# State-space tables made in the down tiles, chunk inputs two rounds ahead in halves, first steps beside the input product

## The reference, cut to what matters

```python
u = rmsnorm(x) @ odd_w_in                   # the input product ("odin")
lam = min(lam_re, -1e-4) + 1j * lam_im      # 128 groups of 64 states
lam_bar = exp(lam * dt)                     # decay and turn of each state per token
b_bar = (lam_bar - 1) / lam * (b_re + 1j * b_im)
h[t] = lam_bar * h[t-1] + b_bar @ u[t]      # per group, 16 channels in and out
y = real(c @ h) * 2 + d_skip * u
out = gelu(y) * sigmoid(gelu(y) @ w_glu + b_glu)
```

## Time and profile before

| what | value |
|---|---|
| median of 3 runs (range) | 4123.23 us (4119.73 to 4124.74) |
| the profiled execution, device time | 4120.54 us |
| its span, first to last instruction | 4119.2 us, mean granted clock 0.973 |
| busy: PE, DVE, ACT, POOL | 93%, 63%, 43%, 36% |
| chain that ended last: PE, DVE, ACT, DMA | 73%, 16%, 7%, 2% |
| layer 0's net, 2017.9 to 2832.7 us | 814.8 us |
| `odin` and state space, 2832.7 to 3072.3 us | 239.6 us |

### The profile page before, as it was taken

The page is one execution under the profiler, slowest core; times in us unless marked ns, Lnnn a source line. Parts: engine busy times, 40 slices in busy tenths (PEclk is TensorE's granted clock), DMA queues, the critical chain, the costliest instruction groups (busy, mean ns, idle before and its releaser), DMA issues.

```text
span 4119.2 us, 66502 instructions
## 1 busy us (share of the span) xinstructions
PE 3835.4 (93%) x28426; PEld 3256.0 (79%) x28426; DVE 2580.1 (63%) x3607; ACT 1788.5 (43%) x2781; POOL 1472.7 (36%) x701
## 2 busy tenths in 40 slices
PE   6898999999999999989899898999869999999998
PEld 3786888787878887888688786888758878888887
DVE  0435743794378897677777767466555866455457
ACT  1435443654355444545534433344334554333334
POOL 0332443243323440024334343444534434444443
PEclk8999999999999999999999999999889999999999
DMA  9653665345534451034345554547325434454543
GB/s 392 270 213 148 263 232 224 141 166 212 210 143 164 164 199 59 3 144 169 132 162 194 186 202 178 210 184 286 145 104 193 175 143 184 184 186 182 198 178 135
DMA packets 60119, 747.66 MB, mean 182 GB/s; under 512 B 6704, under 2 KB 8880, under 8 KB 16176
## 3 DMA queue, kind: packets, MB, share of 16 engines
q1 hardware_dynamic: 48960, 696.74, 44.4%
q0 software_dynamic: 8800, 44.57, 2.7%
q10 hardware_dynamic: 2064, 2.10, 0.1%
HBM read 726.60 MB, written 16.78 MB: 180 GB/s over the span
## 4 chain that ended last, share of the span: by engine, by line
PE 73%; DVE 16%; ACT 7%; DMA 2%; issue 2%; POOL 0%; SPq 0%; another core or an unknown queue 0%; DVEq 0%; ACTq 0%; POOLq 0%
PE ps L370 40%; PE ps L371 20%; DVE pieces L323 3%; ACT pieces L307 3%; DMA ring<-in_ada 2%; PE ps L2229 2%; PE ps L790 2%; DVE scr L3234 1%; DVE scr L592 1%; PE ps L3530 1%; DVE r L1173 1%; DVE scr L382 1%; DVE mix L3229 1%; PE ps L1899 1%; DVE opa L571 1%
## 5 line engine op out<-in xcount | busy, mean ns | idle before, releaser
L370 PE MATMUL ps<-opa,pieces 128*128 128x512 f32 x6192 | 2266.3, 408 | 100.8 <-DVE pieces L323 81.7
L341 POOL TENSOR_TENSOR pieces<-ring,pieces 128x1024 fp32r<-128x1024 f32 x539 | 1340.2, 2487 | 2237.5 <-ACT pieces L307 2219.4
L371 PE MATMUL ps<-opa,pieces 128*128 128x256 f32 x6192 | 1745.6, 282 | 0.0
L370 PEld LDWEIGHTS ps<-opa,pieces 128*128 128x128 f32 x6192 | 1177.3, 190 | 403.7 <-issue 87.7
L307 ACT ACTIVATE pieces<-ring 128x1024 fp32r<-128x1024 f32 (+1 forms) x1110 | 1098.3, 1036 | 830.6 <-PE ps L371 830.0
L371 PEld LDWEIGHTS ps<-opa,pieces 128*128 128x128 f32 x6192 | 1183.2, 191 | 8.9 <-issue 5.3
L370 PE MATMUL ps<-opb,pieces 128*128 128x512 f32 x2560 | 912.6, 398 | 23.6 <-DVE pieces L323 17.9
L323 DVE TENSOR_TENSOR pieces<-ring,pieces 128x1024 fp32r<-128x1024 f32 (+1 forms) x571 | 704.7, 1234 | 294.3 <-ACT pieces L307 290.8
L371 PE MATMUL ps<-opb,pieces 128*128 128x256 f32 x2560 | 726.7, 284 | 0.0
L370 PEld LDWEIGHTS ps<-opb,pieces 128*128 128x128 f32 x2560 | 484.2, 189 | 146.9 <-issue 17.2
L371 PEld LDWEIGHTS ps<-opb,pieces 128*128 128x128 f32 x2560 | 485.0, 189 | 0.1
(11 more groups left out here) (424 smaller groups left out, 3382.2 us busy)
## 6 DMA issues: line engine op xcount, KB each, us to landing
ring<-in_up SPq DMA_DIRECT2D x64, 2048.0 KB, 7.7
ring<-in_down SPq DMA_DIRECT2D x64, 2048.0 KB, 7.8
ring<-in_win SPq DMA_DIRECT2D x56, 2048.0 KB, 7.7
ring<-in_ada SPq DMA_DIRECT2D x48, 2048.0 KB, 12.1
ring<-in_wout SPq DMA_DIRECT2D x24, 2048.0 KB, 7.7
ring<-in_evin SPq DMA_DIRECT2D x18, 2048.0 KB, 7.9
ring<-in_evout SPq DMA_DIRECT2D x8, 2048.0 KB, 7.8
ring<-in_xkv SPq DMA_DIRECT2D x8, 2048.0 KB, 7.7
```

The costliest lines, as they stand in the source:

```text
L341: g.do.tensor_tensor(lo[:, s, :], w[:, s, :], hi[:, s, :].bitcast(F), ALU.subtract).then_inc(*K.lo2.up(p))
L370: pe.do.matmul(b[:, 0:512], hi[:, k, :], op[:, 512 * k:512 * k + 512], start=i == 0, stop=False)
L371: t = pe.do.matmul(b[:, 0:256], lo[:, k, :], half(op, 0, k), start=False, stop=i == kt - 1)
```

## The change

1. Layer 0's net: `next(tables)` on DVE is taken from the up tiles, so tables advance in down tiles of rounds 0 to 2 only (48 slots, table j from slot `first_slot(j)`). The columns run in up tiles of round 0 as eleven short steps behind the tile's own work. Their two 128x2048 products move to ACT as four copies with a scale. ACT writes a whole quarter (two instructions) per tile, from tile `pads_from(j)`; the last table's quarters fall on tiles 96 to 99, the first up tiles of round 3. POOL stores two tiles after each.
2. `odin`: K products follow tiles 0, 3, 6, 9 (before: 1, 4, 8, 10), all from one C buffer, so each load waits for the K before it. in(0) follows tile 11. ACT's turn tables 0 to 2 and DVE's first state steps run beside tiles 13 to 15.
3. State space: in(s) and out(s) are cut into halves with a signal each, in the order in(1), out(0,0), in(2,0), out(0,1), in(2,1), out(1,0), ... The B tables of group 1 are asked for after tile 14.

```diff
 def dve_ffn(K, l):
-    tables = iter(()) if l else dve_s5_beside(K)
+    columns, tables = (iter(()), iter(())) if l else (dve_s5_columns(K), dve_s5_beside(K))
...
-            next(tables, None)
             dve_normed(K, p + n, h, K.rstd, ("usum", l, q, n)).then_inc(*K.dve.up())
...
             dve_part(K, K.opb, ("ho", l, q), n, s)
+            if n >= 2:
+                next(columns, None)
...
-def first_turn(j):
-    return TURN0 + 8 * j + 12 * (j >= 4)
+def first_slot(j):
+    return 6 * j + 6 * (j >= 4)
+def pads_from(j):
+    s = first_slot(j) + 5
+    return 32 * (s // 16) + 16 + s % 16 + 1
...
 def act_s5_columns(K):
+    for c, src in enumerate((K.lre5, K.lim5)):
+        a.wait_ge(*K.dve.of(("lam5", c)))
+        if c:
+            a.wait_ge(*K.prod.of(("row5", 0, 1)))
+        for q in range(2):
+            a.do.activation(rows[:, :, q], src[:, :, None].broadcast_to([P, 64, 16]), ACT.Copy,
+                            scale=K.half5[0][:, q:q + 1]).then_inc(*K.act.up(("wide5", c)))
+            yield
+        yield
...
 def act_s5_pads(K, j):
             a.do.activation(o, i, ACT.Copy, scale=K.half5[which == "b"][:, q:q + 1]).then_inc(*K.act.up(("pad", u)))
-            yield
+        yield
...
-    store = {first_turn(u // 4) + 7 + 2 * (u % 4) + 3: u for u in range(28)}
+    store = {pads_from(u // 4) + u % 4 + 2: u for u in range(28)}
...
 def sp_s5_tables(K):
-    sp.wait_ge(*K.tile.of(K.first["odin"] + 15))
+    sp.wait_ge(*K.tile.of(p + 14))
     load_b(K, sp, 1)
+    sp.wait_ge(*K.tile.of(p + 15))
     load_c(K, sp, 1)
...
-ORDER_K = {1: 2, 4: 3, 8: 0, 10: 1}
+ORDER_K = {0: 2, 3: 3, 6: 1, 9: 0}
...
-        if n == 14:
-            K.pe.wait_ge(*K.act.of(("K", 1)))
-            pe_s5_in(K, 0)
+        if n == 11:
+            K.pe.wait_ge(*K.act.of(("K", 0)))
+            pe_s5_in(K, 0, 0)
+            pe_s5_in(K, 0, 1)
...
 def dve_odin(K):
+        for _ in range(min(n - 12, 2)):
+            next(steps)
+    drain(steps)
...
 def pe_s5(K):
+    K.pe.wait_ge(*K.dve.of(("u", 15)))
+    pe_s5_in(K, 1, 0)
+    pe_s5_in(K, 1, 1)
+    for s in range(4):
+        for h in range(2):
+            pe_s5_out(K, s, h)
+            if s < 2:
+                pe_s5_in(K, s + 2, h)
```

More of the change, by code:

```diff
@@ L3112, in act_s5_columns @@
     a.do.activation(dt, K.col("ldt"), ACT.Exp).then_inc(*K.act.up("dt"))
-    for _ in range(4):
+    for _ in range(5):
         yield
@@ L3119, in act_s5_columns @@
     a.do.activation(sh, th, ACT.Sin, scale=0.5).then_inc(*K.act.up("sh"))
-    for _ in range(8):
+    for _ in range(5):
+        yield
+    a.wait_ge(*K.dve.of("half5"))
+    rows = K.wide5.rearrange("p (j q i) -> p j q i", q=2, i=16)
+    for c, src in enumerate((K.lre5, K.lim5)):
[6 more added lines that the diff above has]
+            yield
         yield
@@ L3278, in act_s5_beside @@
 def act_s5_beside(K):
-    yield from beside(act_s5_columns(K), *(delayed(first_turn(j) + 7, act_s5_pads(K, j)) for j in range(7)))
+    yield from beside(act_s5_columns(K), *(delayed(pads_from(j), act_s5_pads(K, j)) for j in range(7)))
 def dve_s5_beside(K):
-    yield from beside(dve_s5_columns(K), *(delayed(first_turn(j), dve_s5_table(K, j)) for j in range(7)))
+    yield from beside(*(delayed(first_slot(j), dve_s5_table(K, j)) for j in range(7)))
 def delayed(turns, steps):
@@ L3444, in act_odin @@
             a.do.activation(K.K5[:, 384 * s:384 * s + 384], K.bank["K", s][:, 0:384], ACT.Copy).then_inc(*K.act.up(("K", s)))
+        if n >= 13:
+            act_s5_tables(K, n - 13)
 def dve_odin(K):
-    v, p = K.v, K.first["odin"]
+    v, p, steps = K.v, K.first["odin"], dve_s5(K)
     for n in range(16):
@@ L3527, in pe_s5_in @@
             for r in range(4):
-                for q in range(4):
+                for q in qs:
                     q0 = 32 * q
@@ L3546, in pe_s5_out @@
     direct = K.K5.rearrange("p (m k i) -> p m k i", m=16, k=3)
-    for m in range(4):
-        y = K.bank["y5", s, m // 2][:, 256 * (m % 2):256 * (m % 2) + 256]
+    for m in (2 * h, 2 * h + 1):
+        y = b[:, 256 * (m % 2):256 * (m % 2) + 256]
         for z in range(4):
@@ L3562, in pe_s5_out @@
                                      K.p5[4 * s % 8 + q][:, 256 * z + 64 * m:256 * z + 64 * m + 63], start=False, stop=r == 2 and z == 3)
-        if m % 2:
-            t.then_inc(*K.prod.up(("y5", 4 * s + m)))
+    t.then_inc(*K.prod.up(("y5", 4 * s + 2 * h + 1)))
 def act_s5(K):
     a = K.a
-    for n in range(16):
+    for n in range(3, 16):
         act_s5_tables(K, n)
@@ L3598, in dve_s5 @@
             v.wait_ge(*K.dve.of(("w", m)))
+            if m == 0:
+                slab_split(K, v, K.first["odin"] + 15)
             if m >= 8:
@@ L3618, in pool_s5 @@
     g = K.g
[L3619 to L3623, removed]
+    slab_split(K, g, K.first["odin"] + 15)
     for n in range(16):
```

123 lines of the change are left out of this document (56 added, 67 removed).

## The result

| | before | after |
|---|---|---|
| median of 4 runs (range) | 4122.96 us (4119.73 to 4124.74) | 4085.99 us (4079.35 to 4090.44) |
| ratio, 95% interval | | 0.991 (0.9893 to 0.9927) |
| the profiled execution, device time | 4120.54 us | 4090.44 us |
| layer 0's net | 814.8 us | 744.5 us (-70.3) |
| `odin`, first tile's start to tile 15's end | 103.5 us | 127.9 us (+24.4) |

The kernel is faster by 0.9%, 37 us in the medians. The forecast was 4046, 77 us less than before, and the result lies outside its range. The three stretches sum to -36.9. The profiled execution of after also reached layer 0's net 8.3 us later, at 2026.2 instead of 2017.9, in code that is unchanged, and took 1.6 us less from there on behind the state space: -36.9 + 8.3 - 1.6 = -30.2, against 4090.44 - 4120.54 = -30.1.

What follows compares the result with a forecast made beforehand. PE was taken to bound the kernel, with gains only where the chain of waits leaves PE. Net -66.6, input product +4.8 and state space -15.4 gave -77.2: 4043.3 us profiled, 4046 as median, range 4024 to 4070.

Steps and rivals of the forecast that it cites:

- Layer 0's net, -66.6: Layer 0's net: sum of its up and down round terms once table work moves to down tiles, -66.6 us.
- Up rounds 1 and 2: Layer 0's net: without DVE table steps or pads they fall to a plain round's 90.5 us, together -57.5.
- Down round 2: Layer 0's net: falls from 95.9 to 91.0 us, -4.9, as DVE's work stays below PE's.
- Up round 3: Layer 0's net: the last table's quarters make turns late in up tiles, +4.7 us, bounds 1 and 7.
- Up round 0: Layer 0's net: with column work in short steps, 109.8 us against 118.7, -8.9, bounds 102 to 116.
- The stores: Layer 0's net, down rounds: quarters wait for landings of earlier stores, at no cost, bound 2 us.
- held once per down tile with a table step and not twice: Layer 0's net: one hold forecast; rival, chance 0.03, had POOL hold both L323 and the table step: +11, 4134 us.
- K and one C buffer, +4.8: Input product: waits with one C buffer, +1.8 before K2, +2.0 before K3, +1.0 for K1 and K0, together +4.8 us.
- in(0) costs its 7.3 us in either place: Input product, `odin`: the moved in(0) takes the same 7.3 us as before.
- in(1) at full clock: done at 9: State space: in(1) starts near 2 us after X, the end of tile 15, and ends at 9 instead of 21.7.
- a half is about 5: State space: each half of in(2) or in(3) takes about 5 us with issue gaps; whole in(2) took 11.2.
- -15.4: State space: with halves alternating, the last out ends 114 us after tile 15 instead of 129.4; bounds -30 and 0.

Runs made afterwards that it cites:

- experiment 10: experiment 9 with group 3's B tables asked for as soon as in(1) is done, ahead of group 2's C tables: 4038.66 us, ratio 0.9794.
- experiment 11: experiment 10 with six extra 128x128 matmuls, results unused, in PE's pause between tile 15 and in(1): 4041.87 us, ratio 0.9801.
- experiment 1: The changed kernel with in(0) and in(1) each whole over four row groups, in(2) and in(3) still in halves: 4065.43 us, ratio 0.9872.
- experiment 2: The changed kernel with every in(s) whole, in(2) and in(3) behind both halves of out(0) and out(1): 4052.25 us, ratio 0.9836.
- experiment 5: The kernel before with only in(0)'s matmul order changed, row groups 0 and 1 first, then 2 and 3: 4141.55 us, single run.
- experiment 4: The changed kernel with in(0) whole but four calls per row group in a row, and in(1)'s halves writing four banks: 4096.49 us, single run.
- experiment 8: experiment 2 with whole in(2) and in(3) between the halves of out(0) and out(1), second half's results collected later: 4050.09 us, ratio 0.9825.
- experiment 9: experiment 8 with two C buffers, K products behind tiles 1, 4, 8, 10 and in(0) behind tile 13: 4045.96 us, ratio 0.9811.

## Why the prediction was wrong

The direction was right, the size was half. By its own steps:

- **Layer 0's net, -66.6: right, -70.3.** Up rounds 1 and 2: -30.7 and -27.0, together -57.7 for -57.5. Down round 2: 90.8 for 91.0. Up round 3: 94.9, which is 4.5 over a plain round's 90.4, for +4.7. In four of its tiles L592, the scaling, took 1.73 to 1.90 us and ended 0.3 us after POOL's L341; in the first tile, beside no L341, it took 0.43. Up round 0: 107.4 for 109.8, inside its bounds. The stores cost nothing on the path: ACT did stand in its pads for them five times, 4.5 us in all. DVE was held once per down tile with a table step and not twice.
- **K and one C buffer, +4.8: nearly right.** PE stood 3.9 us for ACT's negated B slices, 1.9 before K2 and 2.0 before K1, none before K3. With the 1.6 us that K2 and the tile behind it lost to a lower clock it is 5.5. The wait is not the C table's, though, but that of the B slice that POOL asks for right behind it (13.3 and 14.2 us to land).
- **"in(0) costs its 7.3 us in either place": the failed step, for `odin`.** It cost 23.0, and the tile after it took 7.6 instead of 5.6 at the clock that in(0) left. That is 15.7 + 2.0 of the 24.4; with K's 5.5 it is 23.2.
- **"in(1) at full clock: done at 9" and "a half is about 5": the failed step again, for the state space.** in(1) was done at X + 26.3 (24.9 us of matmuls). The halves of in(2) and in(3) were 10.5 to 11.7. Out(0,0), put at X + 20.9, began at X + 26.2; out(0,1) ended at X + 52 instead of 42.7. The halves of out(0) and out(1) took 7.6 to 7.9 us, less than the 8.4 put, so they are not what failed. The four halves of in took 44.4 where the sum had 20, and the term was +9.0 for -15.4.
- The alternation's gain was real but cost more than it gave as cut. Whole pieces between out's halves give -15.0 in this stretch in experiment 10, the size forecast, but -10.8 in experiment 11 with the same order; the difference is mostly in(2)'s clock, so the agreement with -15.4 is in part luck. It also took the later collecting and the earlier load.

The error has one root. I divided the time of 256 matmuls by two, without asking what made them fast: a loop over four row groups, in which each neighbour works elsewhere in the array. The diff takes two of the four away, in plain sight. The rivals had waits, transfers and instruction gaps, but none where an instruction itself becomes slower. Experiments 1 and 2 take the cause away and give 21 and 34 us back (17 and 30 if each is set against the before beside it), experiment 5 puts it in and loses 20. The Trainium skill (TensorE: Matmul & The Clock Gate, section "Architectural detail: the array is 16× 32×32, not 1× 128×128") states that a matmul in one 32x32 part of the array can run while other parts still load weights. The traces agree in kind: 28 ns with four row groups by turns against 57 with two.

**Still open.** No run shows why the granted clock falls while PE is busy without a gap. In the place of in(0), behind tiles at full clock, it never fell in the ten traces with a whole in(0) in rotation (7.4 us each), and it fell after 4.1 to 5.1 us in all three without it (after, experiments 4 and 5). But four row groups don't keep it up for good: in the whole in(1) of experiments 1, 2 and 8 it fell after 6.4 to 7.5 us, and in(2) of the same kind took 7.9 us at full clock in experiment 10 and 12.5 in 9 and 11. Open too is what a short pause does: after 1.4 us in(1) had full clock for 2.1 us and more, after 1.7 to 2.0 us for 1.0 at most. Each of these is one profiled execution. And why two calls of different row groups come no faster than a row of calls in one group isn't shown either.

## What to carry to other kernels

When a diff cuts a run of small matmuls, look at which loop is innermost before you scale its time: cut along the loop that doesn't rotate through the row groups. The best order of pieces is then found by what DVE waits for at each (here: whole in(2) between out's halves, with its load asked for one step earlier). Move work out of a closed loop between engines into an open one, as the table steps from up to down tiles: that part alone gave more than this change's whole gain, and its size could be read in rows of before.

## What was not expected of the hardware

- A float32 matmul of 32 rows, 128 columns of weights and 64 of data, from start to start: 28 ns with four row groups by turns (in(0) of before), 57 with two (in(0) of after), both at full clock; 53 and 102 at half clock. With four calls in a row in the same group it is 66 (experiment 4). Writing four PSUM banks instead of two changes nothing (56 ns at full clock).
- In a stretch in which PE was 100% busy, on two row groups, the granted clock fell from 1.00 to 0.50 after 4.1 us and stayed there to its end (2850.3 to 2873.3).
- After a pause of 1.7 to 2.0 us behind a product at full clock, in(1) ran at half clock almost from its start (13.1 to 13.6 us). With six dummy calls in the pause it had full clock for 198 of its 256 matmuls.
